# A mixture-of-experts encoder layer: experts run in an order sorted by block count, and their weights issued at other places

## The reference, cut to what matters

```python
lg = jnp.einsum('td,dg->tg', xt, w_rg) + b_rg
pg_top, g_sel = lax.top_k(jax.nn.softmax(lg, axis=-1), 1)      # 1 of 4 groups
le = jnp.einsum('td,gde->tge', xt, w_re) + b_re
le = jnp.take_along_axis(le, g_sel[:, :, None], axis=1)[:, 0]
pe_top, e_sel = lax.top_k(jax.nn.softmax(le, axis=-1), 2)      # 2 of its 8 experts
gate = pg_top * pe_top / jnp.sum(pe_top, axis=-1, keepdims=True)
...
h = jax.nn.silu(xb @ w1[e]) * (xb @ w3[e])
return (h @ w2[e]) * gts[:, None]
```

## Time and profile before

| | |
|---|---|
| median of three runs | 1176.98 us (1174.44 to 1177.91) |
| profiled execution | 1176.07 us |
| its span, first to last instruction | 1174.3 us |
| PE, DVE, ACT, POOL busy | 1010.8, 528.2, 400.5, 266.6 us |
| transfers, mean over the span | 263 GB/s |
| blocks, pieces of expert weights | 62, 96 |

### The profile page before, as it was taken

One profiled execution on the slowest core, in us unless ns is written; L12 is line 12 of the kernel. 1 busy time (PEld: TensorE's weight loads), 2 busy tenths in 40 slices (PEclk: granted clock), 3 DMA queues, 4 the chain that ended last, 5 costly groups with the idle time before them and its releaser, 6 DMA issues. The chain is left out here.

```text
span 1174.3 us, 24283 instructions
## 1 busy us (share of the span) xinstructions
PE 1010.8 (86%) x9062; PEld 703.3 (60%) x9062; DVE 528.2 (45%) x968; ACT 400.5 (34%) x712; POOL 266.6 (23%) x319
## 2 busy tenths in 40 slices
PE   5999999999999999999985885796978788697980
PEld 4888888888876657778873442353544444343540
DVE  5741522211028888555455444344253335253366
ACT  5422233321135666212214252423244233324232
POOL 0110010100100000000001553163563326262440
PEclk9999999999999999999996998797999889897995
DMA  8733331621332004449348999999999999999975
GB/s 315 284 117 126 116 125 45 249 99 45 143 143 91 1 2 161 162 127 380 127 160 337 416 420 419 417 418 422 419 418 418 419 421 419 418 417 420 393 277 217
DMA packets 69427, 308.93 MB, mean 263 GB/s; under 512 B 8376, under 2 KB 8552, under 8 KB 61200
## 3 DMA queue, kind: packets, MB, share of 16 engines
q1 hardware_dynamic: 57008, 273.86, 58.8%
q0 software_dynamic: 12384, 34.63, 7.6%
HBM read 275.68 MB, written 36.44 MB: 266 GB/s over the span
## 5 line engine op out<-in xcount | busy, mean ns | idle before, releaser
L597 PE MATMUL ps<-whi,xTh 128*128 128x512 f32 x480 | 187.5, 391 | 13.8 <-DVE wlo L1253 13.8
L599 PE MATMUL ps<-whi,xTl 128*128 128x512 f32 x480 | 187.2, 390 | 0.0
L598 PE MATMUL ps<-wlo,xTh 128*128 128x512 f32 x480 | 187.2, 390 | 0.0
L886 PE MATMUL ps<-cur13a,xT 128*32 128x256 f32 x1984 | 140.6, 431 | 6.2 <-issue 3.3
L1804 POOL DMA_INDIRECT xg<-xn_scratch,idxb x60 | 95.2, 1586 | 195.4 <-PE ps L875 163.2
L1701 DVE COPY cur13a<-rawe 128x4096 f32 x31 | 71.4, 2302 | 150.9 <-DMA rawe<-in_w 117.9
L886 PE MATMUL ps<-cur13b,xT 128*32 128x256 f32 x1984 | 125.3, 394 | 0.9 <-DVEq L1717 0.5
L910 PE MATMUL ps<-cur,hT 128*32 128x256 f32 x1952 | 118.0, 382 | 7.4 <-issue 7.0
L1216 ACT ACTIVATE cur<-rawe 128x4096 f32 x30 | 108.6, 3621 | 8.4 <-DMA rawe<-in_w 4.3
L986 ACT ACTIVATE zst<-ps,rstd 128x512 f32<-128x512 f32 x60 | 40.8, 687 | 204.4 <-PE ps L599 197.1
L597 PEld LDWEIGHTS ps<-whi,xTh 128*128 128x128 f32 x480 | 90.5, 189 | 32.6 <-issue 13.8
(11 more groups left out here) (219 smaller groups left out, 1338.7 us busy)
## 6 DMA issues: line engine op xcount, KB each, us to landing
rawe<-in_w SPq DMA_DIRECT2D x96, 2048.0 KB, 31.2
raw<-in_w_in SPq DMA_DIRECT2D x20, 1024.0 KB, 8.2
z_scratch<-zst POOLq DMA_DIRECT2D x60, 256.0 KB, 2.3
gat<-z_scratch SPq DMA_DIRECT2D x12, 512.0 KB, 3.9
xn_scratch<-rrow POOLq DMA_DIRECT2D x6, 1024.0 KB, 5.0
raw<-in_w_out SPq DMA_DIRECT2D x4, 1024.0 KB, 6.7
xcol<-in_x_cols SPq DMA_DIRECT2D x6, 512.0 KB, 9.9
x_scratch<-x SPq DMA_DIRECT2D x6, 512.0 KB, 3.2
```

What stands on the lines that cost most here:

```text
L597: pe.matmul(out, ah, bh, start=first, stop=False)
L598: pe.matmul(out, ah, bl, start=False, stop=False)
L599: return pe.matmul(out, al, bh, start=False, stop=last)
L886: mm = pe.matmul(ps[0][u * CAP:(u + 1) * CAP, 0:256], xT[:, c % 2, x:x + CAP], cur13[h][:, :, c * 512 + u * P:c * 512 + (u + 1) * P], star ...
```

## The change

There are four parts.

1. **Order of the experts.** ORDER becomes (0, 1, 2, 3). Position p in round 1 (p < 4) stays expert 0 of its group. From round 2 on, the experts of each group run by falling block count. A table made on the chip says which: `key` (8 times the padded count and a rank for ties), `place` (how many of the group have a greater key), `put_at` (one-hot), `sorted_w`, from which `ends` and `first` now come, and `first_of`, which takes them back to the experts' own numbers. `eid` holds the number of the expert at each position, and SP reads it with a register load ahead of each expert from position 4 on.
2. **Weights.** SP issues position 1's w2 and position 2's w1 when ten of twelve halves of the projection are done, then x2 of the last two tiles, then position 1's w1 and w3 and position 2's w3, then position 2's w2 when all rows are normalised, and position 3 next. The wait for the first gather is gone.
3. **Projection.** The last two tiles are interleaved: the first half of tile 4, the first of tile 5, the second of 4, the second of 5. Tile 3's transposes and logits stand inside the first of these, tile 4's inside the last. The last tile's logits go to bank 5. DVE and the thresholds on `s_x2` follow (X2_DONE).
4. **Places.** The routing's scratch tensors move so that ACT can fill cur13b before the routing is over; ACT copies cur13b, then cur13a, then cur2, this last one behind `s_nb`. `Rt` now lies on `rrow[0]`, so the first one_hot waits for its stores. `Bt` lies on xg, so POOL clears xg when the last product of the table is done. The gates' operations on DVE come behind the first xT.

```diff
-ORDER = (2, 0, 1, 3)
+ORDER = (0, 1, 2, 3)
...
+        X2_DONE = [2 * t + 2 for t in range(NT - 2)] + [2 * NT - 1, 2 * NT]
...
-            for t in range(NT - 1):
+            for t in range(NT - 2):
                 sp.wait_ge(s_x2, 2 * t + 2)
                 x2_out(t)
...
-            sp.wait_ge(s_w, 2 * NT)
-            expert(1, EPG * ORDER[1])
-            sp.wait_ge(s_x2, 2 * NT)
+            sp.wait_ge(s_w, 2 * NT - 2)
+            weight(EPG * ORDER[1], 1, 2, s_w2)
+            weight(EPG * ORDER[2], 2, 0, s_w1)
+            sp.wait_ge(s_x2, X2_DONE[NT - 2])
+            x2_out(NT - 2)
+            sp.wait_ge(s_x2, X2_DONE[NT - 1])
             x2_out(NT - 1)
+            weight(EPG * ORDER[1], 1, 0, s_w1)
+            weight(EPG * ORDER[1], 1, 1, s_w3)
+            weight(EPG * ORDER[2], 2, 1, s_w3)
             sp.wait_ge(s_rr, NT)
-            weight(EPG * ORDER[2], 2, 0, s_w1)
-            sp.wait_ge(s_gx[0], 16)
-            weight(EPG * ORDER[2], 2, 1, s_w3)
             weight(EPG * ORDER[2], 2, 2, s_w2)
-            for p in range(3, 8):
-                expert(p, EPG * ORDER[p % NG] + p // NG)
+            expert(3, EPG * ORDER[3])
+
+            def number(p):
+                return sp.value_load(eid[0:1, p:p + 1] if isinstance(p, int) else eid[0:1, bass.ds(p, 1)],
+                                     min_val=0, max_val=EPG - 1)
+            sp.wait_ge(s_nb, 1)
+            for p in range(4, 8):
+                expert(p, EPG * ORDER[p % NG] + number(p))
...
-                mm = pe.matmul(ps[2][:, 0:NG + NE], rT[:, c, :], wrt[:, c, :],
+                    mm = pe.matmul(ps[5 if t == NT - 1 else 2][:, 0:NG + NE], rT[:, c, :], wrt[:, c, :],
...
+            merged_to_columns(NT - 1)
+            a, b = NT - 2, NT - 1
+            project(a, 0, 6, 2 * a - 1, {1: lambda: route_columns(a - 1), 5: lambda: logits(a - 1)})
+            project(b, 0, 7, 2 * a)
+            project(a, 1, 6, 2 * a + 1)
+            project(b, 1, 7, 2 * a + 2, {1: lambda: route_columns(a), 5: lambda: logits(a)})
             route_columns(NT - 1)
...
             act.wait_ge(s_w1[0], 16)
             act.wait_ge(s_w3[0], 16)
+            first_up(1)
             act.wait_ge(s_lg, NT)
...
             first_up(0)
...
+            act.wait_ge(s_nb, 1)
             act.activation(cur2[:, :], rawe[:, 4 * PIECE:6 * PIECE], ACT.Copy).then_inc(s_cw2, 1)
...
-            act.wait_ge(s_nb, 1)
-            first_up(1)
...
-            link(dve.tensor_tensor_scan(ends[:, :], wide[:, :], zero[:, :], 0.0, ALU.add, ALU.add))
-            link(dve.tensor_tensor(first[:, :], ends[:, :], wide[:, :], ALU.subtract))
...
+            link(dve.scalar_tensor_tensor(out=key[:, NG:], in0=wide[:, NG:], scalar=8.0, in1=C("erank")[:, NG:],
+                                          op0=ALU.mult, op1=ALU.add))
+            link(dve.tensor_tensor(prod4, key[:, :].rearrange("p (j g) -> p j g", g=NG).unsqueeze(3)
+                                   .to_broadcast([P, EPG, NG, EPG]), by_group(key), ALU.is_lt))
+            link(dve.tensor_reduce(place[:, :], prod3, AX.X, ALU.add))
...
+            link(dve.tensor_tensor(prod4, put_at[:, :, :, :], by_group(wide), ALU.mult))
+            link(dve.tensor_reduce(sorted_w[:, :], prod3, AX.X, ALU.add))
+            link(dve.tensor_tensor_scan(ends[:, :], sorted_w[:, :], zero[:, :], 0.0, ALU.add, ALU.add))
...
+            link(dve.tensor_reduce(first_of[:, :], prod3, AX.X, ALU.add))
...
+            dve.wait_ge(s_rst[0], 16 * NT // 2)
             for q in range(NT):
                 one_hot(q)
...
             pool.sem_inc(s_is, 1)
+            pool.wait_ge(s_tbm, 2 * NT)
             for k in range(2):
                 pool.memset(xg[k][:, :], 0.0).then_inc(s_zr, 1)
```

More of the change, by code:

```diff
@@ L155, in hybrid_layer @@
     served = small("served", [1, NB], I32)
+    eid = small("eid", [1, NE], I32)
     bcol = small("bcol", [P, 8])
@@ new lines, in project @@
+            def project(t, n, bank, free, at_step={}):
+                pe.wait_ge(s_mTl, 2 * t + 2)
+                if free > 0:
+                    pe.wait_ge(s_x2, free)
+                for c in range(KC):
+                    p, k = 2 * n + c // 4, c % 4
+                    if t == 0 and k == 0:
+                        pe.wait_ge(s_lo, ZP + 4 + p + 1)
+                    mm = split_mm(ps[bank][:, :], mTh[t % 2][:, c, :], mTl[t % 2][:, c, :],
+                                  m_hi[4 + p][:, k * 512:(k + 1) * 512],
+                                  m_lo[4 + p][:, k * 512:(k + 1) * 512],
+                                  c == 0, c == KC - 1)
+                    if c in at_step:
+                        at_step[c]()
+                mm.then_inc(s_w, 1)
@@ new lines, in _ @@
+            merged_to_columns(0)
+            for t in range(NT - 2):
+                merged_to_columns(t + 1)
+                project(t, 0, 6, 2 * t - 1)
+                if t >= 1:
+                    route_columns(t - 1)
+                project(t, 1, 7, 2 * t, {3: lambda: logits(t - 1)} if t >= 1 else {})
+            merged_to_columns(NT - 1)
+            a, b = NT - 2, NT - 1
+            project(a, 0, 6, 2 * a - 1, {1: lambda: route_columns(a - 1), 5: lambda: logits(a - 1)})
+            project(b, 0, 7, 2 * a)
@@ L1580, in _, with add_residual, row_for_experts @@
             BIG = 1.0e30
-            for t in range(NT):
-                if t + 1 < NT:
-                    merged_lo(t + 1)
-                else:
-                    choose(0, NT - 2)
-                dve.wait_ge(s_xr[t % 3], 16 * (t // 3 + 1))
-                for n in range(2):
-                    dve.wait_ge(s_w, 2 * t + n + 1)
-                    if t >= 3 and n == 0:
-                        dve.wait_ge(s_rTm, 2 * (t - 2))
-                        dve.wait_ge(s_x2s[t % 3], 16)
-                    dve.tensor_tensor(x2[t % 3][:, n * 512:(n + 1) * 512], ps[6 + n][:, :],
-                                      xres[t % 3][:, n * 512:(n + 1) * 512], ALU.add).then_inc(s_x2, 1)
+            def add_residual(t, n, bank, done):
+                if n == 0:
+                    dve.wait_ge(s_xr[t % 3], 16 * (t // 3 + 1))
+                dve.wait_ge(s_w, done)
+                if t >= 3 and n == 0:
+                    dve.wait_ge(s_rTm, 2 * (t - 2))
+                    dve.wait_ge(s_x2s[t % 3], 16)
+                dve.tensor_tensor(x2[t % 3][:, n * 512:(n + 1) * 512], ps[bank][:, :],
+                                  xres[t % 3][:, n * 512:(n + 1) * 512], ALU.add).then_inc(s_x2, 1)
+            def row_for_experts(t):
                 dve.wait_ge(s_sq2, t + 1)
```

139 lines of the change are left out of this document (73 added, 66 removed).

## The result

| | before | after |
|---|---|---|
| median | 1176.49 us (1174.44 to 1177.91) | 1163.49 us (1160.92 to 1164.94) |
| span of the profiled execution | 1174.3 us | 1161.7 us |

The ratio is 0.9888, with a 95% interval of 0.9865 to 0.9912: 13 us faster. Predicted were 1162 us, in a range of 1150 to 1172.

The account below looks back on a forecast made before the run. Weight transport was taken to bound the expert phase. Last sigmoid 16.1 us sooner (1121.5 against 1137.6) and tail +1.5 turn the 1174.3 span into 1159.7, profiled 1161.5, median 1162 us; range 1150 to 1172.

Parts of the forecast that it names:

- What bounds: Expert phase: transport of weights bounds it, 5.38 us a piece, gathers and stores included; start and end are not transport-bound.
- Rival A: Rounds 2 to 4: PE becomes the bound, its backlog uses up the ring's room, queue held 7 to 10 us; 1172, chance 0.10.
- Projection: Last two tiles interleaved: one new stall, 0.5 us; last logits in bank 5, their DVE operation near 616.6, gain 1.6 us.
- The table: DVE ahead of the slot numbers: eight instructions +3.5 us, loose ends +0.3; idxt net +2.2, at 638.2.
- POOL and the gather: First gather issued near 639.8, landing after 7 us (2.7 to 8.3), first up product at 648.3.
- rival C: First gather lands in under 3 us, DVE's chain to expert 1's copies is quicker; 1154, chance 0.15.
- rival D: First gather stands behind all weights in the queue, 24 us more than taken; 1186, chance 0.10.
- The queue: SP's weights issued near 597, 612, 620; expert 4's w1 at 658.7, losing 8 us of early start to the ring.
- From there: Expert 4's w1 to expert 31's w3: 82 pieces of 5.38 us, +2 for gathers and stores, to 1111.2; last sigmoid +10.3.
- The split: Of 16.1 us at the last sigmoid, 6.3 come from an earlier last w3, about 9.9 from PE backlog the order removes.
- The tail: After the last sigmoid: x2t, gf and ye queue behind the last weights; +1.5 us, 0 to 3 possible.
- The clock: PE's last rounds run partly at 1.2 GHz; if the last down product does too, 2 us more.

Follow-up runs that it names:

- three_first: Changed kernel with group order 2, 0, 1, 3 as in the kernel before, still sorted; 1174.09 us, 0.9969 of the kernel before.
- warm: Changed kernel with six filler products on PE instead of three while it waits for the first gather; 1163.50 us, 0.9877 of the kernel before.
- both: Changed kernel with gates' operations ahead of the first xT, six fillers, and expert 3's w3 issued behind the first gathers; 1158.70 us, 0.9858 of before.
- table_twice: Changed kernel with the ten table operations on DVE, from key to first_of, run twice in a row; 1165.27 us, 0.9900 of the kernel before.
- gates_early: Changed kernel with the thirteen gates' operations on DVE moved ahead of the first xT, and six fillers on PE; 1160.94 us, 0.9854 of before.
- tail_more: Changed kernel with two more unused loads of 512 KB ahead of x2t in SP's queue; 1164.21 us, 0.9897 of the kernel before.
- halves: Changed kernel with w1 and w3 fetched in pieces of 1 MB, each with its own wait and signal; 1164.74 us, 0.9885 of the kernel before.
- start_only: Changed kernel with block counts taken out of the sorting key, so experts of each group run by number; 1174.32 us, 0.9974 of the kernel before.
- after_again: The changed kernel measured once more, unaltered, beside the combination of two edits on the same chip; 1162.56 us, 0.9884 of the kernel before.
- order_only: Changed kernel keeping the table, with weights issued where the kernel before issued them; 1170.40 us, 0.9943 of the kernel before.
- gather_then: Changed kernel with expert 3's w3 issued only when POOL has issued both first gathers; 1160.16 us, 0.9862 of the kernel before.
- gather_ahead: Changed kernel with expert 3's w3 to wait for POOL's first gather, though SP still issued it first; 1162.42 us, 0.9870 of before.

## Why the prediction was right, and where it was not

**What bounds.** Right in the main, too simple in the middle. DMA share is 1.0 from 660 to 1113, and six of the last eight copies wait for weights (4.7 to 10.4 us of idle time). But over the first four rounds the pace is set by the engines: the 226.0 us between the first copy and the one for position 16 don't change by 0.1 us, and by three_first the weight for position 16 was there some 8 us before its copy. Most rows there name a DMA or PE as releaser, with 2.4 to 3.4 us of idle time. warm shows for the first of them that it was neither; the others up to position 16 have the same lengths within 0.1 us in both and table_twice, whatever name stands there; that they are DVE's register loads too is inferred. The first wait beyond that is at 903.98, for position 18. Rival A, the backlog of PE, was right that the blocks set the pace there (PE is busy 188 of 200 us from 700 to 900). The ring's room was enough, as forecast, and there is no second dip.

**Projection.** The stall was 1.3 us, not 0.5: the last half's residual runs at 611.29, where it was at 609.95. The last logits are at 616.99, against 616.6 forecast.

**The table.** Eight operations, forecast 3.8 us. Three of them and the step behind, on DVE:

```profile
624.23 0.60 DVE L1656 TENSOR_TENSOR t<-key 128x256 f32<-128x256 f32 x1
624.86 0.42 DVE L1658 TENSOR_REDUCE place<-t 128x32 f32<-128x256 f32 x1
625.32 0.59 DVE L1659 TENSOR_TENSOR put_at<-place,cst 128x256 f32<-128x256 f32 x1
628.62 0.36 DVE L1669 TENSOR_TENSOR t<-ps,first_of 128x192 f32<-128x192 f32 x1
638.70 0.28 DVE L1713 TENSOR_SCALAR idxt<-ps,cst 128x80 int32<-128x80 f32 x1
```

An operation of 256 elements takes 0.59 to 0.62 where one of 384 took 0.56: scaling by the element count was wrong for these strided reads. The reductions at 0.42 make up for it. From wint to this step it is 5.26 us, 1.14 before: 4.1. idxt came at 638.70, 0.5 late. What table_twice adds, and the prediction lacked: of a delay there more than half vanishes, as the gather then lands faster.

**POOL and the gather.** Issue 640.22 (639.8 forecast), landing 7.0 us (7 taken), first product 648.42 (648.3). The landing was my least certain number and was chosen from one row. Landing in under 3 us (rival C) needs an idle queue, and 31 us (rival D) occurs nowhere: 4.6 to 7.1 us in eleven kernels with weights in the queue. The Trainium skill ("DMA: Bandwidth & Descriptors", Queues, rings and completion order) has each engine take turns between its queues, which I had read as a landing near 3. The runs don't agree with that reading: the gather does not wait for the whole of SP's queue, as the rule says, but it pays 2 to 4 us for company.

**The queue.** Pieces at 597.67, 612.38, 621.17 (597, 612, 620), expert 1's copies done at 658.81 (658.7), expert 4's w1 issued at 658.99. The 8 us called lost to the ring were 5.1 us of idle transport. three_first, gates_early and both confirm the mechanism from both sides: first copies 10.9 us later give a last copy 9.3 later, 2.1 sooner 3.0, 3.1 sooner 4.1 (two profiles of the changed kernel itself differ by 0.8 there).

**From there.** 454 us from expert 4's issue to the last copy, forecast 452.5: 1112.66 instead of 1111.2. The allowance of 2 us for gathers and stores was a little small. Copy to last sigmoid 10.14 (10.3 taken).

**The split** into 6.3 us from weights and 9.9 from the order was the step that failed. Without the other part, and with parts 3 and 4 counted in, they are 2.8 and 7.8 at the last sigmoid. My 9.9 was taken with the early start in place, and the 6.3 at a last weight that PE's backlog would have hidden. With the other part in place the runs give 7.0 for the weights and 12.0 for the order, which add to 19 and not to 14.8. So 6.3 and 9.9 add up as steps of one path from before to after, but not as the worth of each part.

**The tail.** +2.2, taken as +1.5. The last sigmoid to the end is 38.9 us (36.7 before), and I had kept one term of it: ya's issue 9.3 us after the last sigmoid. It is 11.2. The last store into y_scratch and the first load of ya, before (see the earlier trace rows for ya) and after:

```profile
1143.26 2.08 POOL L1825 DMA_INDIRECT y_scratch<-ystage,idxs  x1 [1.12 <-ACT ystage L1195]
1128.48 0.98 POOL L1876 DMA_INDIRECT y_scratch<-ystage,idxs  x1 [1.43 <-ACT ystage L1209]
1133.97 3.30 SPq L597 DMA_DIRECT2D ya<-y_scratch  x6
```

The store comes 5.7 us after the last sigmoid in both kernels, but ya, which waits for the store, follows 5.5 us later where it was 3.6: 1.9 of the 2.2 us. From ya's issue to DVE's first use of it are 4.5 us in both. The loads of x2t, gf and ye now stand behind the weights and are in the queue at that time; that they hold the store up is likely but not shown, since tail_more adds its 2.0 us between ya's issue and its use (7.0 us). In every kernel whose weights last to the end the last sigmoid to the end is 38.8 to 40.2 us (halves 42.3, tail_more 41.2), and 36.9 in start_only. Of the 2.0 us by which the span exceeds the forecast 1159.7, 1.3 are the last sigmoid's and 0.7 the tail's.

**The clock.** The first product ran at a granted clock of 0.64 to 0.68, part of it at 1.2 GHz, 3.64 us for 1.93, and cost nothing. The last one cost 1.7 us:

```profile
1117.39 3.61 PE L902 MATMUL ps<-cur13a,xT 128*32 128x256 f32 x32 [0.81 <-issue]
```

and in table_twice:

```profile
1118.54 1.93 PE L902 MATMUL ps<-cur13a,xT 128*32 128x256 f32 x32 [0.77 <-issue]
```

Over 1117 to 1122 the granted clock is 0.66 in the first and 1.00 in the second. The same instructions stand ahead of it on PE in both, but not the same idle time. The transpose of hh ahead of it, in the changed kernel and in table_twice:

```profile
1116.25 0.33 PE L910 MATMUL ps<-cst,hh 128*128 128x128 f32 x1 [1.30 <-DVE hh L1730]
1117.43 0.33 PE L910 MATMUL ps<-cst,hh 128*128 128x128 f32 x1 [0.92 <-DVE hh L1744]
```

The kernels sort by this: PE was idle there for 1.30, 1.29, 1.39 and 6.13 us in after, after_again, warm and three_first, whose product took 3.54 to 3.63 us, and for 0.92 us or less in the nine others and the kernel before, where it took 1.93 or 1.94. No run changed that idle time on purpose. The last sigmoid is 10.1 us behind the copy in the first four, and 8.4 or 8.5 in start_only, order_only, table_twice, gates_early and both. In gather_then, tail_more and gather_ahead (8.7 to 9.0) the product was fast too, but began 4.9 to 5.3 us after the copy and not 4.7. That my 10.3 us fitted is in part luck: it was measured behind a slow product (3.64 us at 1073.03 in the kernel before, where PE had been idle for 7.4 us). The Trainium skill ("TensorE: Matmul & The Clock Gate", HAM oscillation) says bursts between DMA waits start at the lower clock; for the last up product that holds in some of these runs, for the last down product, of which I had made 2 us more, in none that I read (1.93 us in the changed kernel and in both).

## What to carry to other kernels

Where the end is the later of two chains (weights in, blocks worked off), changes to one of them are worth little alone, so price them together and test them apart. A prefetch ring is worth what its first release allows: put the shortest work first, and look for small operations that stand ahead of the copy that frees the first slot. And when a releaser in a row costs the same few microseconds again and again, add work or take it away there, as the fillers did, before believing its name.

## What was not expected of the hardware

- A gather of 128 rows that is ready 4.1 us later can be there only 1.7 us later: 7.0 us from issue among the weights, 4.6 when the queue was just running empty (DMA share 0.76 at 646 to 648), 2.9 with an idle queue, 5.6 to 6.1 with one piece moved behind it, 6.2 among pieces of 1 MB. What in the queue sets this stays open, since moving 5 us of traffic took off only 0.9 to 1.4 us.
- Pieces of 1 MB, 8 KB to a partition and row, moved 414 GB/s where pieces of 2 MB moved 418, over 700 to 900 us (415 and 419 over 900 to 1060).
- The same product, with the same instructions ahead of it, took 3.6 us in four profiles and 1.9 in the others, and they sort by whether PE had been idle for 1.3 us or for 0.9 just ahead. That is 1.7 us at the last sigmoid. From the last copy to the end it is 48.9 to 49.6 us with the slow product and 47.2 to 48.6 with the fast one (halves, start_only and tail_more left out, whose tails differ).
